# Attention of a two-block transformer kernel: queries scaled in place, another negated maximum, separate PSUM banks, score products over 64 partitions

## The reference, cut to what matters

```python
def windowed_gqa(q, k, v, sink):          # layer 0: 12 query heads, 4 key heads
    s = einsum('bnikgd,bnukd->bkgniu', qb, kband) * D ** -0.5      # blocks of 128 queries, up to 384 keys
    s = where(allowed, s - slopes * dist, NEG_INF)
    p = softmax(concatenate([s, sink_col], -1), -1)[..., :-1]
    return einsum('bkgniu,bnukd->bnikgd', p, vband)
def neighbourhood_attn(q, k, v, rpb):     # layer 1: 12 query and 12 key heads
    s = einsum('brchd,brijhd->bhrcij', qg, kband) * D ** -0.5 + bias
    p = softmax(where(in_win, s, NEG_INF), -1)
    return einsum(p, vband)
def memory_attn(q, k, v):                 # both layers: 4 heads, 256 memory tokens
    p = softmax(einsum('bshd,bmhd->bhsm', q, k) * D ** -0.5, -1)
    return einsum('bhsm,bmhd->bshd', p, v)
```

## Time and profile before

| what | value |
|---|---|
| median of 3 runs | 2225.71 us (2225.0 to 2227.97) |
| the profiled execution's own time | 2229.44 us |
| its span in the profile | 2227.7 us |
| PE busy | 2119.3 us, 95% of the span |
| DVE, ACT, POOL busy | 1096.6, 832.0, 262.4 us |
| instructions | 33476 |
| mean granted TensorE clock | 0.976 |
| attention of layer 0, of layer 1 (first score to last value) | about 1053 to 1138 us, 1684 to 1779 us from the span's start |

### The profile page before, as it was taken

One profiled execution on the slowest core, in us unless ns is written; L12 is line 12 of the kernel. 1 busy time (PEld: TensorE's weight loads), 2 busy tenths in 40 slices (PEclk: granted clock), 3 DMA queues, 4 the chain that ended last, 5 costly groups with the idle time before them and its releaser, 6 DMA issues.

```text
span 2227.7 us, 33476 instructions
## 1 busy us (share of the span) xinstructions
PE 2119.3 (95%) x11856; PEld 1828.6 (82%) x11856; DVE 1096.6 (49%) x1781; ACT 832.0 (37%) x1301; POOL 262.4 (12%) x263
## 2 busy tenths in 40 slices
PE   6998999988999999999999999999998999999997
PEld 6988888878998898887878888888886878888886
DVE  4223666645565366644755443444247654433443
ACT  4433333353322344443743321334434633322322
POOL 1004222210010010001200100110005100100100
PEclk8999899999999999999999999999999999999998
DMA  3322110113333233242003333333322023332331
GB/s 107 96 87 76 39 37 29 38 48 100 95 94 97 83 94 96 84 123 85 1 20 95 94 103 86 94 105 95 94 76 53 18 60 96 96 103 86 95 100 64
DMA packets 321757, 174.71 MB, mean 78 GB/s; under 512 B 6544, under 2 KB 318992, under 8 KB 321696
## 3 DMA queue, kind: packets, MB, share of 16 engines
q1 hardware_dynamic: 321696, 173.92, 27.0%
HBM read 171.80 MB, written 2.10 MB: 78 GB/s over the span
## 4 chain that ended last, share of the span: by engine, by line
PE 63%; DVE 3%; issue 1%; ACT 1%; POOL 0%; DMA 0%; ACTq 0%; DVEq 0%; POOLq 0%; SPq 0%
PE ps L1708 54%; PE ps L2088 2%; PE ps L2064 2%; PE ps L2046 2%; PE ps L2073 1%; DVE neg_max L1677 1%; PE ps L2119 0%; DVE mix_lo L1683 0%; DVE ls L1605 0%; PE ps L2133 0%; DVE w_lo L1084 0%; ACT mix_hi L1061 0%; PE ps L1785 0%; DVE pts L1623 0%; ACT w_hi L682 0%
## 5 line engine op out<-in xcount | busy, mean ns | idle before, releaser
L1084 DVE TENSOR_TENSOR w_lo<-raw,w_hi 128x1024 fp32r<-128x1024 f32 (+2 forms) x298 | 386.9, 1299 | 585.2 <-ACT w_hi L682 584.0
L1708 PE MATMUL ps<-z_hi,w_hi 128*128 128x512 f32 (+2 forms) x2192 | 660.1, 343 | 10.3 <-POOL z_lo L607 2.4
L1708 PE MATMUL ps<-z_lo,w_hi 128*128 128x512 f32 (+2 forms) x2192 | 653.8, 340 | 0.0
L1708 PE MATMUL ps<-z_hi,w_lo 128*128 128x512 f32 (+2 forms) x2192 | 651.3, 339 | 0.0
L682 ACT ACTIVATE w_hi<-raw 128x1024 fp32r<-128x1024 f32 (+2 forms) x298 | 328.1, 1101 | 519.1 <-PE ps L1708 459.4
L1708 PEld LDWEIGHTS ps<-z_hi,w_hi 128*128 128x128 f32 x2192 | 379.4, 190 | 66.2 <-issue 11.0
L1708 PEld LDWEIGHTS ps<-z_lo,w_hi 128*128 128x128 f32 x2192 | 377.7, 190 | 45.8
L1708 PEld LDWEIGHTS ps<-z_hi,w_lo 128*128 128x128 f32 x2192 | 377.7, 190 | 45.7
L607 POOL TENSOR_TENSOR g_lo<-gv,g_hi 128x512 f32 x66 | 85.6, 1297 | 1103.8 <-ACT g_hi L933 1103.8
L1708 PE MATMUL ps<-g_lo,w_hi 128*128 128x512 f32 x528 | 209.0, 396 | 0.0
L1708 PE MATMUL ps<-g_hi,w_hi 128*128 128x512 f32 x528 | 207.6, 393 | 0.5 <-POOL g_lo L607 0.5
(11 more groups left out here) (285 smaller groups left out, 2403.4 us busy)
## 6 DMA issues: line engine op xcount, KB each, us to landing
raw<-w_gate_up SPq DMA_DIRECT2D x88, 512.0 KB, 3.8
raw<-w_down SPq DMA_DIRECT2D x48, 704.0 KB, 4.5
raw<-w_in SPq DMA_DIRECT2D x44, 512.0 KB, 3.8
raw<-w_up SPq DMA_DIRECT2D x44, 512.0 KB, 3.8
raw<-w_out SPq DMA_DIRECT2D x24, 512.0 KB, 3.7
raw<-w_in_b SPq DMA_DIRECT2D x14, 512.0 KB, 3.8
raw<-w_in_a SPq DMA_DIRECT2D x12, 512.0 KB, 3.7
raw<-w_branch SPq DMA_DIRECT2D x8, 512.0 KB, 3.6
```

What stands on the lines that cost most here:

```text
L1084: dve.tensor_tensor(w_lo[s][:, 0:width], raw[s][:, 0:width], w_hi[s][:, 0:width].bitcast(F32), ALU.subtract).then_inc(lo_done, 1)
L1708: x = pe.matmul(out, w[s][:, w0 + k * P:w0 + (k + 1) * P], rhs[:, lo:lo + width], start=a, stop=b)
```

## The change

It does seven things:

1. The 12 token queries are scaled by DVE in place, in `scaled(m)`, like the keys. `q_now`, POOL's `queries`, the waits on them and all the zeroing go.
2. Each score product takes 64 partitions of queries and keys instead of 128.
3. `neg_max` is made by a SCALAR_TENSOR_TENSOR with two tensor inputs in SBUF: (max of row_max and sink) times a constant tile `minus`, or -2 row_max + row_max.
4. The value products get banks of their own (`v_bank`): `ps[0]` and `ps[3]` in layer 0 and in half 1 of layer 1; `ps[2]` and `ps[1]` in half 0 of layer 1, where only the last bank waits for the projection's copies. The copies signal semaphores of their own (`va`, `vd`), for which the first value product of the attention waits.
5. The turn goes through seven banks (`turn_bank`), the eighth group uses the first again; the `out` gemm waits tile by tile for `mix_lo`.
6. `head_steps` is written out in full, and POOL makes its first bias earlier, at the start of the projection.
7. In the branch stage of the first block DVE's `split_lo` moves behind `zt`.

The diff, cut to its core:

```diff
+        minus = sb(fixed, "minus", [P, 4])
-        q_now = [sb(at, "q_now0", [P, SEQ])]
+        def v_bank(l, half, c):
+            if l == 0 or half:
+                return ps[(0, 3)[c // 2]][:, c % 2, :]
+            return ((ps[2], 0), (ps[2], 1), (ps[1], 1), (ps[1], 0))[c][0][:, (0, 1, 1, 0)[c], :]
+        def turn_bank(k):
+            i, b = ((2, 0), (2, 1), (3, 0), (3, 1), (0, 1), (1, 1), (1, 0), (2, 0))[k]
+            return ps[i][:, b, :]
...
-            for h in range(3):
-                step(h, h, h, 0)
-            with eng.Fori(0, QH // 3 - 1) as g:
...
-            for h in range(QH, AH + 3):
+            for h in range(AH + 3):
                 step(h, h % 3, h, h // 3)
... POOL
+                pool.wait_ge(used, UNITS[("mem", "qk1")[l]] + 2)
                 pool.wait_ge(att_loaded, 16)
-                pool.wait_ge(*norm_a[l].at("copied", 1))
-                def queries(h, r):
...
                 biases(0, 0, 0)
...
-                queries(0, 0)
                 pool.wait_ge(used, UNITS[f"out{l}"] + 2)
-                for h in (1, 2):
-                    queries(h, h)
-                    biases(h, 0, h)
...
+                for h in range(1, QH):
+                    biases(h, h // 3, h % 3)
... ACT
-                        x = act.activation(v_tok[...], ps[0][:, c, 0:width],
-                    x.then_inc(ps_free[0], 1)
+                        x = act.activation(v_tok[...], v_bank(l, half, c)[:, 0:width],
+                    x.then_inc(atts[l]["va"], 1)
... DVE, branch stage
-                    split_lo(n + m + 2, s)
                     dve.wait_ge(used, n + m + 3)
...
                     dve.tensor_tensor(zt[s][:, :], ta[:, :], tb[:, :], ALU.add).then_inc(brs["mixed"], 1)
+                    split_lo(n + m + 2, s)
... DVE, projection
+                    if m < first_key:
+                        tiles = q_heads[0:HD, 2 * m:2 * m + 2, :]
...
-                dve.memset(q_heads[HD:, QH:, :], 0.0)
-                dve.memset(q_now[0][HD:, :], 0.0)
... DVE, attention
-                        dve.tensor_scalar(neg_max[r][:, :], row_max[r][:, :], vec("sink", h), -1.0,
-                                          ALU.max, ALU.mult).then_inc(s["neg"], 1)
+                        dve.scalar_tensor_tensor(neg_max[r][:, :], row_max[r][:, :], vec("sink", h), minus[:, :],
+                                                 ALU.max, ALU.mult).then_inc(s["neg"], 1)
                     elif front:
-                        dve.tensor_scalar(neg_max[r][:, :], row_max[r][:, :], -1.0, 1.0, ALU.mult, ALU.mult)\
-                           .then_inc(s["neg"], 1)
+                        dve.scalar_tensor_tensor(neg_max[r][:, :], row_max[r][:, :], -2.0, row_max[r][:, :],
+                                                 ALU.mult, ALU.add).then_inc(s["neg"], 1)
... PE, values
-                        if i == 0:
-                            pe.wait_ge(ps_free[0], freed[0] + 1 + half)
-                            pe.wait_ge(ps_free[1], freed[1] + 1 + half)
+                    if l == 0 or half:
+                        pe.wait_ge(ps_free[0], freed[0] + 1)
+                    if l == 0:
+                        pe.wait_ge(fin_x, KD)
...
+                                    if l and not half and c == 3 and a:
+                                        pe.wait_ge(ps_free[1], freed[1] + 1)
... PE, attention
+                    q = q_heads[0:HD, n_, b * P:(b + 1) * P]
                     if memory:
-                        q, keys = q_heads[:, n_, b * P:(b + 1) * P], mk[:, MH * l + n_ - QH, :]
+                        keys = mk[0:HD, MH * l + n_ - QH, :]
                     else:
-                        q, keys = q_now[r][:, b * P:(b + 1) * P], k_heads[:, bass.ds(kv, 1), lo:lo + width]
+                        keys = k_heads[0:HD, kv, lo:lo + width]
... PE, turn and out
                 for k in range(KD):
-                    pe.wait_ge(ps_free[k % 2], FREED[f"turn{l}"][k % 2] + 1 + k // 2)
+                    if k == 7:
+                        pe.wait_ge(*s.at("lo", 1))
...
-                gemm(f"out{l}", SEQ, 4, mix_hi, mix_lo)
+                gemm(f"out{l}", SEQ, 4, mix_hi, mix_lo, KD, lambda k: pe.wait_ge(*s.at("lo", k + 1)))
```

More of the change, by code:

```diff
@@ L329, in build @@
                            + [x for l in range(2) for x in
-                              [(f"qk{l}", (5, 7)[l], (5, 7)[l]), (f"v{l}", (1, 2)[l], (1, 2)[l]),
-                               (f"turn{l}", 4, 4), (f"out{l}", 4, 4)]
+                              [(f"qk{l}", (5, 7)[l], (5, 7)[l]), (f"out{l}", 4, 4)]
                               + [(f"{w}{l}_{h}", c, c) for h in "ab" for w, c in (("up", FH), ("down", 4))]]):
@@ L1018, in layer @@
                     for c in range(2):
-                        x = act.activation(v_tok[:, c, half * width:(half + 1) * width], ps[0][:, c, 0:width],
-                                           ACT.Identity, scale=token_scale(l, c))
-                    x.then_inc(ps_free[0], 1)
+                        x = act.activation(v_tok[:, c, half * width:(half + 1) * width],
+                                           v_bank(l, half, c)[:, 0:width], ACT.Identity, scale=token_scale(l, c))
+                    x.then_inc(atts[l]["va"], 1)
                     m = count * (half + 1) - 1
@@ L1060, in layer @@
                     act.wait_ge(*s.at("turned", k + 1))
-                    act.activation(mix_hi[:, k, 0:SEQ], ps[k % 2][:, 0, :], ACT.Copy).then_inc(s["hi"], 1)
+                    act.activation(mix_hi[:, k, 0:SEQ], turn_bank(k), ACT.Copy).then_inc(s["hi"], 1)
                 residual_squares(f"out{l}", SEQ, norm_f[l], lambda k: vec("ffn_g", KD * l + k))
@@ L1090, in _ @@
             lb1 = par[:, pc["lb1"]:pc["lb1"] + 8]
+            dve.memset(minus[:, :], -1.0)
             dve.tensor_tensor(lbc[:, 2, :], lb0, lb1, ALU.max).then_inc(lb_step, 1)
@@ L1583, in layer @@
                     dve.wait_ge(used, n + count * (half + 1) + 2)
-                    if half == l:
-                        dve.memset(q_now[1][HD:, :], 0.0)
-                        dve.memset(q_now[2][HD:, :], 0.0)
-                    for c in range(2):
-                        x = dve.tensor_scalar(v_tok[:, 2 + c, half * width:(half + 1) * width], ps[1][:, c, 0:width],
-                                              token_scale(l, 2 + c), 1.0, ALU.mult, ALU.mult)
-                    x.then_inc(ps_free[1], 1)
+                    for c in range(2, 4):
+                        x = dve.tensor_scalar(v_tok[:, c, half * width:(half + 1) * width],
+                                              v_bank(l, half, c)[:, 0:width], token_scale(l, c), 1.0,
+                                              ALU.mult, ALU.mult)
+                    x.then_inc(s["vd"], 1)
                     m = count * (half + 1) - 1
@@ L2086, in values @@
                         else:
-                            v = v_tok[:, block, bass.ds(kv * HD, HD)]
+                            v = v_tok[:, block, kv * HD:(kv + 1) * HD]
                         x = pe.matmul(y_bank(r)[:, b * HD:(b + 1) * HD], pts[b % 2][:, j * P:(j + 1) * P], v,
```

66 lines of the change are left out of this document (26 added, 40 removed).

## The result

The kernel after takes 2393.4 us in the median (2392.5 to 2394.9), the kernel before 2226.8 us in the same session: a ratio of 1.0749, 95% interval 1.0731 to 1.0768. I had forecast +4.4 us with an upper end of 2243 us; it is +167 us. In the terms of my signs of being wrong, the granted clock is at 0.5 in both attentions. The profiled execution took 2394.0 us, with a span of 2392.2 us.

A forecast was written before the change was run, and what follows sets the result against it. PE, busy for 95% of the span, was taken as the bound. Gains of 39.2 us against a cost of 43.6 us gave net +4.4 us, a median of 2230.1 us; range 2217 to 2243 us, leaving out the clock and the free product.

The forecast's parts named there:

- my signs of being wrong: Heads of 5.3 us, PEclk at 0.5 within an attention, layer 1 maximum above 1 us, or a gap moved elsewhere.
- The sum: Whole kernel: gains 39.2 us against cost 43.6 us, net +4.4 us; nil at 0.36 us a score product.
- The clock falls: Rival, both attentions: half rows and more gaps leave 14 heads at half clock, +75 us, about 2305 us; chance 0.04.
- The change of form: Attention score products: entering and leaving the 64-partition form costs 0.40 us each, 112 of them, +44.8 us.
- The rival that the form is no change: Score products: 64 partitions cost nothing, heads 5.29 us in both layers, 2186.5 us; chance 0.12.
- the branch stage: First block: `zt` moved ahead of the weight split removes PE's waits for `zt` and the last `mix_lo`, -6.0 us.
- from there to the first transposes: Attention starts and value products: layer 0 -1.5, -2.6, -1.7 us; layer 1 -2.0, -0.5, -1.3, -0.8 us.
- layer 1's attention: POOL's query work goes, the maximum takes 0.17 us, seven head periods fall from 6.42 to 5.29 us: -7.9 us.
- the turns: From first transposes to the gemm, each layer: seven banks let PE issue 32 transposes in 3.6 us; -7.2 and -6.4 us.
- the gemm behind the second: Layer 1's gemm, 2.7 us longer than layer 0's, at half clock after the gaps: -1.3 us.
- The maximum: Layer 1's negated maximum: new form alone buys nothing, POOL's shorter work does; DVE assumed first, 0.17 us.
- The rival that it still waits: POOL's bias starts first, layer 1's maximum waits 2.4 us, heads 7.2 us: +3 us, about 2233 us; chance 0.04.

The follow-up runs named there:

- first2z: Kernel after with score products over 128 partitions in steps 0 and 1 only, POOL's zeroing of query rows put off four projection units: 2226.0 us, ratio 0.9985.
- late64: Kernel after with score products over 128 partitions in steps 0 to 3, 64 from step 4 on: 2226.3 us, ratio 0.9991.
- first2: Kernel after with score products over 128 partitions in steps 0 and 1 alone, 64 from step 2 on: 2232.4 us, ratio 1.0014.
- k128: Kernel after with score products over 128 partitions again, upper query rows zeroed by POOL: 2193.1 us, ratio 0.9835.
- k65: Kernel after with score products over 65 partitions, query row 64 zeroed by POOL: 2332.8 us, ratio 1.0476.
- zlater: `k128` with POOL's zeroing of the query rows put off by four units of the projections: 2184.8 us, ratio 0.9802.
- oldmax: `k128` with the negated maximum in its old form, one input tensor instead of two: 2190.0 us, ratio 0.9831.
- d128: Kernel after with score products over 128 partitions, except each block's last 32 columns in a separate product over 64: 2333.8 us, ratio 1.0471.
- pause64: `late64` with DVE held back by two groups of memsets in step 7, ahead of the second and third block: 2323.9 us, ratio 1.0420.
- early64: Kernel after with score products over 64 partitions in steps 0 to 3, 128 from step 4 on: 2223.4 us, ratio 0.9975.
- half64: Kernel after with score products over 64 partitions in blocks 1 and 3 of each head, 128 in blocks 0 and 2: 2222.4 us, ratio 0.9986.
- gap128: `k128` with DVE held back once by four memsets ahead of the maximum of step 7: 2192.3 us, ratio 0.9834.

## Why the prediction was wrong, point by point

**The clock, the step that failed.** The sum had no term for the clock: it stood at nothing, and it is worth 167 us, by `first2z` against the kernel after. The rival "The clock falls" had the clock's fall in it and got a chance of 0.04; that half rows keep the clock from coming back, it did not say. I argued against it that "pauses here are 0.1 to 0.2 us long". That is true of full running, and there it was right: `late64` and `first2` keep 1.00 with all these pauses. I did not ask it of the start of the attention. The kernel before had longer pauses there already, 2.30 us in layer 0, 2.57 and 1.85 us in layer 1:

```profile
1687.59 2.52 PE L2064 MATMUL ps<-k_heads,q_now 128*128 128x256 f32 x8 [1.85 <-DVE row_max L1605]
```

Behind them, over 128 partitions, its clock stayed at 1.00. In the kernel after PE idles for 1.56 us between its first score products, over 64 partitions too, and what follows decides whether a fallen clock comes back. In `k128`, with much the same start over 128 partitions, the clock is at 1.00 there in layer 0 and dips for 3 to 4 us in layer 1. I had seen PE run for 3.5 us at half clock after a pause of 2.47 us and took from it that the clock comes back by itself, which a stretch of products over 128 partitions could not show for 64. The rival's size was wrong too: I let half of both attentions run at twice a head's 5.29 us, +75 us. It was all of both, at 12.61 us a head, of which 10.24 us are the streams at half clock (by `k65`) and 2.37 us four changes of form at 0.59 us.

The Trainium skill, TensorE: Matmul & The Clock Gate, Part 1, ties half clock to an idle PE and full clock to a busy one. The trace of the kernel after does not agree with that, if busy is what the profile shows as busy: 120 of 120 us busy at 0.50. What the engine's time is filled with counted here, not that it is filled.

**The change of form, right.** Forecast 0.40 us a score product from a 16*128 product of another stage; measured 0.39 us by head periods and 0.38 us by time at full clock. The rival that the form is no change is out. The sum was to turn at 0.36 us, and at that it was a close call, as forecast.

**The gains, low by 4 to 6 us.** Forecast 39.2 us; `zlater` is 45.6 us faster than the kernel before by the medians, 43.2 us by the two spans. By stages, forecast against its trace: up to the end of `qk0` (the branch stage) 6.0 against 5.8; from there to the first transposes 5.8 against 4.0; the same in layer 1, 4.6 against 7.0; layer 1's attention 7.9 against 8.5; the turns 13.6 against 7.1 + 6.3 = 13.4; the gemm behind the second 1.3 against 3.0. The sum came near in part because its errors cancel: layer 1's start gave 2.4 us more and layer 0's 1.8 us less than forecast. The turn's 32 transposes take 3.71 us, where I had said 3.6; the 6.15 us of the kernel after are the same work at half clock.

**The sum, near where the clock stays.** `first2z` is the kernel that I computed: 4.3 us faster than before by the medians where I said 4.4 us slower. The cost, `first2z` against `zlater`, is 41.2 us for 112 score products (0.37 each), forecast 43.6; the rest is the gains. With the clock kept up, the change would have been no different from the kernel before, or a hair faster (0.05 to 0.26%), not slower.

**The maximum, right.** The form buys nothing (`oldmax`), POOL's shorter work does, and DVE comes first, as I had assumed without a row: 0.18 us. The rival that it still waits is out for layer 1. In layer 0 it does wait for POOL's bias, 0.72 us on average in `k128`, beside a full PE.

**The range** reached to 2243 us because I left this rival out of it by its small chance. With one row that shows a clock fallen after a pause, and an attention that begins with a pause, it should have had a good deal more.

## What to carry to other kernels

Look at what PE does right after each of its pauses, not only at the pauses: a loop that holds full clock can be unable to regain it. Test a narrower product for this by its clock row, and if it falls, give the first steps behind the pause all 128 rows, or keep the rows at zeros throughout: here a product over 128 partitions with zeros took no longer than one over 64 at the same clock, and the kernel with the zeros was 209 us faster. The best kernel of this study, `zlater`, is the change without its narrow products: 2184.8 us, 2.0% faster than before (1.8 to 2.2%).

## What the runs showed of the hardware that I had not expected

- The granted clock depends in this kernel on what came before. One and the same loop ran at 1.00 and at 0.50 (`d128`, two layers; `pause64`, before and after a pause of 2.12 us).
- It was held down by half rows without changes of form (`k65`), and by changes of form with nearly all rows at work (layer 1 of `d128`, where each block has a product of 32 columns over 64 partitions). It came back with 128 rows (`early64`, after 4 us), and with 64 rows in every second block (`half64`, after 10 and 14 us); with 96 rows it did not fall in either attention. What quantity the chip looks at is not settled by these runs.
- A pause of PE alone did not always lower it: 0.86 us did not (`gap128`), 1.76 us did in `zlater` and did not in `k128`, 0.97 us before products of which some are over 64 partitions did (`d128`).
- 65 and 96 partitions are no change of form against 128 (5.30 us a head with 65 and with 96, 5.29 with 128); 64 partitions are.
- A change into and out of 64*128 costs 0.39 us at full clock and 0.59 us at half clock.
- A 128x4 instruction of DVE with one input took 5.24 us beside POOL's zeroing and 0.17 us without it. The ones ahead of it in the chain (a read of PSUM, a reciprocal, two with two inputs in SBUF) took 0.16 to 0.18 us each while POOL was already at it. The Trainium skill, SBUF — State Buffer, "SBUF: two separate sides", has it that DVE and GpSimd lock each other out of a shared pair of ports for whole instructions, that two SBUF inputs on DVE's side matter only against a GpSimd instruction that reads SBUF, and that DVE's two-port mode matters against any. The zeroing reads nothing; the trace agrees if the waiting instruction is in that mode, which no row names.
